# VectorE's order in a two-block transformer kernel: one sum moved ahead of a tap, and the long convolution's taps dealt out differently

## The reference, cut to what matters

```python
proj = einsum('bsd,de->bse', rms_norm(x, norm_g), w_in)
(a_q, a_k, a_v, a_z, m_q, m_k, m_v, m_o, m_z, m_i, m_f, c_a, c_b, c_z) = split_columns(proj)
qk = silu(causal_depthwise_conv(concat([m_q, m_k]), ml_qk_conv_w, ml_qk_conv_b))   # width 4
hm = mlstm_chunkwise(m_q, m_k, m_v, i_pre, f_pre)      # gates: scans over m_i and m_f
u = causal_depthwise_conv(c_a * sigmoid(c_b), cv_dw_w, cv_dw_b)                    # width 31
cv = silu(layer_norm(u)) * silu(c_z)
```

## Time and profile before

| | us |
|---|---|
| median of 3 runs | 3367.67 (3367.03 to 3368.46) |
| the profiled execution | 3364.18 |
| its span in the profile | 3362.6 |
| TensorE busy | 3231.2 |
| VectorE busy | 1950.9 |
| GpSimd busy | 1706.8 |

### The profile page before, as it was taken

The page is one execution under the profiler, slowest core; times in us unless marked ns, Lnnn a source line. Parts: engine busy times, 40 slices in busy tenths (PEclk is TensorE's granted clock), DMA queues, the critical chain, the costliest instruction groups (busy, mean ns, idle before and its releaser), DMA issues. The chain is left out here.

```text
span 3362.6 us, 43705 instructions
## 1 busy us (share of the span) xinstructions
PE 3231.2 (96%) x16157; PEld 2632.0 (78%) x16157; DVE 1950.9 (58%) x2345; ACT 1240.3 (37%) x1871; POOL 1706.8 (51%) x1142
## 2 busy tenths in 40 slices
PE   5989999999999999999999999999999999898999
PEld 5767878888888778888878888888777788577887
DVE  8687355555555766793456555555758678355511
ACT  5323353333333443312343333333444312566511
POOL 5812856666666326542865556666523742244521
PEclk9999999999999999999999999999999999999999
DMA  6364111111111213323311111111212232425653
GB/s 233 115 132 133 51 52 56 50 50 50 54 52 50 94 44 125 119 101 134 113 60 48 53 50 50 50 54 52 94 48 103 94 122 99 178 79 181 209 149 105
DMA packets 156942, 309.90 MB, mean 92 GB/s; under 512 B 16752, under 2 KB 92016, under 8 KB 154112
## 3 DMA queue, kind: packets, MB, share of 16 engines
q1 hardware_dynamic: 140640, 265.88, 24.4%
q10 hardware_dynamic: 16160, 42.08, 3.3%
HBM read 234.98 MB, written 72.94 MB: 92 GB/s over the span
## 5 line engine op out<-in xcount | busy, mean ns | idle before, releaser
L2137 PE MATMUL ps_job<-AHL,WH 128*128 128x512 f32 x3072 | 951.6, 391 | 16.6 <-POOL WL L1531 10.0
L1531 POOL TENSOR_TENSOR WL<-WR,WH 128x1024 fp32r<-128x1024 f32 x170 | 427.0, 2512 | 770.8 <-ACT WH L1123 769.1
L2137 PEld LDWEIGHTS ps_job<-AHL,WH 128*128 128x128 f32 x3072 | 578.7, 189 | 141.2 <-POOL WL L1531 14.1
L2137 PE MATMUL ps_job<-AHL,WL 128*128 128x512 f32 x1536 | 599.8, 391 | 0.0
L1123 ACT CAST WH<-WR 128x1024 fp32r<-128x1024 f32 x214 | 225.0, 1052 | 752.7 <-PE ps_job L2137 509.3
L2137 PEld LDWEIGHTS ps_job<-AHL,WL 128*128 128x128 f32 x1536 | 289.8, 189 | 60.5
L1833 DVE SCALAR_TENSOR_TENSOR ps_job<-ps_job,RB 128x1024 f32<-128x1024 f32 (+1 forms) x80 | 79.9, 1017 | 405.6 <-PE ps_job L2137 396.1
L1592 POOL TENSOR_TENSOR OPS_L<-VS,OPS_H 128x1024 fp32r<-128x1024 f32 (+2 forms) x96 | 193.5, 2030 | 55.9 <-ACT OPS_H L1312 51.3
L2286 PE MATMUL ps_job<-OPS_H,WH 128*128 128x512 f32 x512 | 199.5, 390 | 0.7 <-POOL WL L1531 0.7
L2286 PE MATMUL ps_job<-OPS_L,WH 128*128 128x512 f32 x512 | 199.3, 389 | 0.0
L2286 PE MATMUL ps_job<-OPS_H,WL 128*128 128x512 f32 x512 | 199.3, 389 | 0.0
(11 more groups left out here) (535 smaller groups left out, 7209.3 us busy)
## 6 DMA issues: line engine op xcount, KB each, us to landing
WR<-in_wall SPq DMA_DIRECT2D x244, 512.0 KB, 3.3
fm_scratch<-VS ACTq DMA_DIRECT2D x32, 512.0 KB, 3.1
tm_scratch<-VS ACTq DMA_DIRECT2D x24, 512.0 KB, 2.7
s_Win<-in_x_chunk SPq DMA_DIRECT2D x8, 1024.0 KB, 7.9
s_U<-in_x_group SPq DMA_DIRECT2D x8, 1024.0 KB, 12.4
s_mt<-z_scratch SPq DMA_DIRECT2D x64, 128.0 KB, 4.6
prod_scratch<-s_Win SPq DMA_DIRECT2D x16, 512.0 KB, 2.6
X<-in_x_feat SPq DMA_DIRECT2D x2, 4096.0 KB, 15.8
```

The source lines that it names most:

```text
L1531: pool.tensor_tensor(dst, raw, src.bitcast(F32), ALU.subtract).then_inc(raw_free, 1)
L2137: last = pe.matmul(out, l, r, start=(k == 0 and i == 0), stop=(k == k_tiles - 1 and i == 2))
```

## The change

The table of taps is dealt out differently. Jobs 18 and 19 keep three taps each; jobs 20 to 23 get two in place of five, jobs 24 to 27 get four in place of five, and jobs 28 to 31 get eight. The sum is 62 as before.

In the pairs, `evict` takes a function that it calls after the second of the three taps of L2014 (k = 1), and `pair` hands it `third_sum`. So the third sum of pair i stands ahead of the last tap of the tile before, and no longer behind it. In the first pair, which evicts nothing, nothing moves.

```diff
-TAPS_AT = {j: 3 for j in range(18, 20)} | {j: 5 for j in range(20, 32)}
+TAPS_AT = {j: 3 for j in range(18, 20)} | {j: 2 for j in range(20, 24)} | {j: 4 for j in range(24, 28)} | {j: 8 for j in range(28, 32)}
...
-                def convolve(j, i):
+                def convolve(j, i, between=None):
...
                         if k:
                             step(ins)
+                        if k == 1 and between:
+                            between()
                     ins.then_inc(conv_out, 1)
...
-                def evict(j):
+                def evict(j, between=None):
                     if KINDS[j] == "conv":
-                        convolve(j, j - M_QK.start)
+                        convolve(j, j - M_QK.start, between)
                     else:
+                        if between:
+                            between()
                         slot_free(j)
...
                     if i:
-                        evict(j - 1)
-                    third_sum(n, FM, slots[1])
+                        evict(j - 1, lambda: third_sum(n, FM, slots[1]))
+                    else:
+                        third_sum(n, FM, slots[1])
                     first_tile(n, FM, slots[0])
```

## The result

| | us |
|---|---|
| before, median of 9 runs | 3367.03 (3365.11 to 3368.46) |
| changed, median of 9 runs | 3374.39 (3372.76 to 3378.59) |
| ratio | 1.0025, 95% interval 1.0014 to 1.0035 (+4.7 to +11.8 us) |
| profiled execution, before and changed | 3364.18 and 3376.28 |

The change makes the kernel 7.4 us slower by the medians. The forecast was +9.1 us and 3376.8 us.

The account below looks back on a forecast made before the run. TensorE, busy 96% of the span, was taken as the bound, so time changes only where it stands still. -6.2 - 4.3 + 17.7 + 1.9 = +9.1 us on 3367.7 gave 3376.8 us, range 3371.5 to 3382.5 us.

Parts of the forecast that it names:

- Part A: Feature-major pairs: third sum ahead of the last tap removes TensorE's wait, -6.2 us, bounds -7 and -3.9.
- Rival 3: Pairs stay at about 20 us, their gain 2 us instead of 6.2: 3381 us, chance 0.05.
- Part B: Token-major jobs 20 to 27: fewer taps remove four waits of the gate-column transposes, -4.3 us, bounds -3.9 and -5.2.
- Part C: Behind job 27's eviction: 36 taps instead of 21 delay block 1's scans, TensorE stands still 17.7 us more; block 0 hidden.
- The clock: After the stop at the scan's ends: TensorE restarts at half speed, +1.9 us, bounds 0 and 4 us.
- rival 1: Waits behind the stop, such as 7.1 us for the row parts, shrink and give it back: 3357.2 us, chance 0.05.
- rival 2: A draw: half the stop given back, or scans some 8 us sooner than forecast; 3367 us, chance 0.05.
- The sum: Whole kernel: pairs, gate transposes, stop and half clock together make it +9.1 us, 0.27% slower.

Follow-up runs that it names:

- block0_only: Changed kernel, but block 1 keeps the old table of taps: 3359.06 us beside 3365.72 for the kernel before, ratio 0.9979.
- taps_only: Kernel before with the new table of taps, third sum left where it was: 3383.08 us, ratio 1.0048.
- tail27: Kernel before with the third sum moved and a table leaving 27 taps behind job 27's eviction: 3365.68 us beside 3365.72, ratio 0.9999.
- sum_only: Kernel before with the third sum moved, old table of taps kept: 3364.03 us beside 3367.42, ratio 0.9993.
- spread_only: Kernel before with another table, 21 taps still behind job 27's eviction, third sum not moved: 3362.85 us, ratio 0.9992.
- tail21: Kernel before with the third sum moved and another table, 21 taps still behind job 27's eviction: 3355.69 us, ratio 0.9968.
- scans_early: Changed kernel and its table, but block 1's constants and gate scans stand behind job 29's taps: 3354.83 us beside 3365.72 before, ratio 0.9964.

## Why the prediction was right, point by point

- *Part A, the pairs.* Forecast 19.03 us a pair in both blocks, -6.2 us; the trace has 19.04 and -6.1 us. The room to spare, 0.3 us by the forecast, was 0.41 us. VectorE's circle fitted, and the work queued behind the moved sum cost nothing. Rival 3 did not come.
- *Part B, the gate transposes.* Forecast -4.3 us; the trace has -2.28 and -2.31. A listed wait of 1.0 us was worth 1.15.
- *Part C, the long row.* Forecast that the scan ends 55.62 us behind job 27's eviction; it ended 55.62 us behind it. Forecast stop 17.8 us, measured 17.72. That the clashes with GpSimd's last four tiles (8.5 us) would be the same ones held: the row took 51.58 us for a forecast 51.6. In both kernels four of the row's first five taps are listed 3.3 to 3.4 us long and all others 1.27 to 1.28. That GpSimd is the cause is read from the two falling together in time; no run here takes its tiles away. The up to 3.5 us more that the prediction worked out from the Trainium skill, page "SBUF — State Buffer", section "Who interferes with whom" (12.0 us of clashes in place of 8.5), did not appear. They could hardly have: the same four operations lay against the same taps before, and what they cost was already in the measured 33.65 us. Block 0 hid its long row altogether, shown by block0_only.
- *The clock.* Forecast +1.9 us; measured +2.11 here, +2.93 behind the equal stop of taps_only and +2.86 behind the shorter one of tail27. The mechanism was right; the size rests on when the clock comes back, which varies, so that the close hit is in part luck.
- *Rivals.* The stop was not given back (rival 1): the wait for the row parts is 7.1 us in every kernel here, with the stop and without it, and the changed kernel is as late at the end of its span (+12.0 us) as behind job 31 (+11.82). The draw (rival 2) did not come either, with 51.6 us for the 36 taps. But its condition was put too high: scans 8 us sooner mean 36 taps in 51.6 - 8 = 43.6 us and not in 42, and at the undisturbed 1.195 us they take 43.0. It needed the clashes gone, not faster taps.
- *The sum.* +9.2 us by the trace for a forecast +9.1. The medians say +7.4, and the interval of the ratio holds both. What parts the two isn't shown.

## What to carry to other kernels

Count an engine's work not only between the waits that you see but up to the next thing that another engine takes from it: here the taps were moved out of the way of two small waits, behind the last eviction, where nothing seemed to wait for them, and pushed the scans that stood behind them in the program. Where two engines meet within 0.3 us, as here, an engine that runs its program in order has no slack left for more work ahead of that point, whatever its busy share (58%). The remedy was not fewer taps but their order: either none added to the last row, or the scans ahead of it; both versions are faster than either kernel.

## What the runs showed of the hardware that was not expected

The time that TensorE ran at 1.2 GHz after a stop did not go with the length of the stop. Behind the changed kernel's 17.7 us it ran some 4.6 us at half clock (to about 2859.3), behind tail27's 7.0 us some 6.3 us (to about 2851.9). Behind the 17.7 us of taps_only, a stop of the same length, it was some 6.4 us (to about 2866.6):

```profile
2860.22 0.26 PE L2990 MATMUL ps_job<-ident,m_row_E 64*1 64x64 f32 x1 [17.71 <-DVE m_row_E L2962]
...
2869.03 0.27 PE L2995 MATMUL ps_job<-ident,m_ends 1*64 1x1 f32 x2
```

```profile
2864.20:2866.20 2.00, 2.00 (x6) 1.55 (x5) 0.00 (x0) 0.00 (x0) 0.00 (x0) 0.50 0.00 0
2866.20:2868.20 2.00, 2.00 (x9) 1.63 (x8) 0.00 (x0) 0.00 (x0) 0.00 (x0) 0.90 0.00 0
```

That is 8.81 us from the first transposes to those behind the job, 2.93 more than without a stop, where the changed kernel had 2.11 more. The same shows where no kernel differs: at the start of the recurrence every one of them waits 7.1 us for the row parts. Windows of the kernel before, then of sum_only, both begun about 6 us ahead of that stage's first matmul:

```profile
3058.00:3068.00 10.00, 3.71 (x15) 3.55 (x16) 6.34 (x15) 3.05 (x8) 2.67 (x4) 0.72 0.72 210
3068.00:3078.00 10.00, 8.50 (x65) 7.59 (x64) 4.45 (x12) 6.67 (x22) 2.99 (x3) 0.94 0.80 275
```

```profile
3053.50:3063.50 10.00, 3.70 (x15) 3.55 (x16) 6.34 (x15) 3.05 (x8) 2.68 (x4) 0.60 0.75 218
3063.50:3073.50 10.00, 8.50 (x53) 7.57 (x52) 3.46 (x10) 5.62 (x18) 1.42 (x2) 0.72 0.77 267
```

The first has 65 matmuls in its second window, at a granted clock of 0.94, the other 53, at 0.72. From the stage's first to its last matmul on the row parts it is 92.4 us in the kernel before and 94.0 us in sum_only. The nine profiles fall into two sorts, 92.4 to 92.5 us (before, changed, spread_only, tail21, scans_early) and 93.7 to 94.1 us (sum_only, taps_only, block0_only, tail27), with the same instructions in all. In the first layer of block 1, block0_only and tail27 lose 3.1 and 3.2 us against before; there too the clock is lower (0.90 in tail27's window 2605 to 2615, 1.00 in that of before); how much of the loss is the clock's was not worked out. There is one profile of each kernel, so it isn't shown that such steps come and go between executions of one kernel; the sorts follow none of the edits, though. Steps of 1 to 3 us in places that no edit touches are why gains of 5 us want the trace beside the medians.
